# Third down product moved ahead of the fourth up product, TensorE's block loop turned by half a block, and the last block taken out of the loop

## The chip, the core and the metric

The kernel runs on one core of a Trainium2 chip. The metric is device time in microseconds (us) of one execution. Three runs of the kernel before took 1391.1, 1392.65 and 1392.87 us; the median is 1392.65 us.

## The reference

One layer of a streaming encoder over 512 tokens of width 1024, with 16 learned meta tokens in front. After the attention half comes a mixture of 32 experts, and the change lies in this second half:

```python
def clamped_swiglu(hu):
    gate, lin = hu[..., :D_FF], hu[..., D_FF:]
    gate = jnp.minimum(gate, SWIGLU_LIMIT)
    lin = jnp.clip(lin, -SWIGLU_LIMIT, SWIGLU_LIMIT)
    return gate * jax.nn.sigmoid(SWIGLU_ALPHA * gate) * (lin + 1.0)

def moe(h, w_router, b_router, w1, b1, w2, b2):
    ...
    top_val, top_idx = lax.top_k(logits, TOP_K)          # 4 of 32 experts for each token
    gates = jax.nn.softmax(top_val, axis=-1)
    ...
    def expert_block(args):
        tok, e = args
        xb = xf[tok]
        act = clamped_swiglu(xb @ w1[e] + b1[e])
        return act @ w2[e] + b2[e]
```

The weighted results are added to the token rows, and a final RMS norm gives the output. `w1[e]` is 1024 x 2048 and `w2[e]` is 1024 x 1024, both float32: 8 MB and 4 MB for each expert, all of them read once.

## The kernel before, in words

**Blocks.** The tokens of an expert are cut into blocks of 32 rows. With the given inputs there are 81 blocks, numbered 0 to 80 (`nb` is 81; the page of the profile counts 81 of the instruction on L1308, which runs once for each block). Experts stand in an order worked out on the chip; an expert's position in it is its *place*, 0 to 31. Place 0 holds three blocks here (0, 1 and 2), place 1 two (3 and 4), place 2 three (5, 6 and 7), and the last place one (block 80).

**Weights.** Two sets of buffers in SBUF hold the weights of an even place and of an odd place (`par` 0 and 1). A place's weights come in six transfers of 2 MB, issued by the SP queue strictly in order: four quarters of w1 (L508) and then two halves of w2 (L513). Each waits until TensorE has read the same part of the place two before for the last time: quarter c of w1 for `w1_read`, which an up product raises four times; the first half of w2 for `w2_read`, which a down product raises in its middle; and the second half for `y_done`, which it raises at its end. A transfer that waits holds up all behind it in the queue.

**One block's work.** GpSimd gathers 32 token rows (`gather`, L600). VectorE turns them to the layout TensorE needs (`turn_rows`, L1255, into the one buffer `xT`). TensorE forms the up product (`up`, L1816, 64 instructions, and the bias products on L1826) in a PSUM bank. VectorE and ScalarE apply the clamped SwiGLU (`hidden`, L1308 to L1314, and `sigmoid`, L849). VectorE turns the result into the one buffer `actT` (`turn_hidden`, L1301). TensorE forms the down product (`down`, bias on L1846, 64 instructions on L1854). VectorE and ScalarE scale it (`outputs`, `high_outputs`), and GpSimd adds it to the rows in DRAM (`scatter`, L609). The last two blocks are not scattered: their rows stay in SBUF (`quarters_kept`, L1321) and are spread by one-hot products after the loop (L1906).

**Lists.** For each block a small chain makes the list of its tokens: VectorE compares (`slot_list`, L1217 and L1221), TensorE sums (`slot_product`, L1786), VectorE makes the indices (`slot_rows`, L1236 to L1249).

**Order on TensorE.** Written u for up, d for down and s for slot_product, the order is u0 u1 u2 d0 d1 u3, and then a loop over pairs of blocks in which `pe_block(g)` is s(g+3), d(g), u(g+2). `up_of` and `down_of` choose by a branch between code for an even and for an odd place (L1833, L1862), each some 130 instructions long. The loop has a fixed number of rounds, for the largest number of blocks that could be (MAXBLK is 95). Rounds past the last block only test (L1894) and count (L1892).

**Order on VectorE.** `dve_block(g)` is hidden(g+1), which also turns the rows of block g+2, slot_rows(g+3), turn_hidden(g+1), outputs(g), quarters_kept(g), slot_list(g+4), selector(g+2). `selector` fills a small tile that TensorE's bias products read.

**After the loop.** TensorE waits for `hot_ready` (the one-hot tiles of `last_places`) and for `y_kept`, and runs the 64 products on L1906. The sums with the rows that came back from DRAM, the norm and the output follow.

Of the kernel before, what the change touches and what calls it, by code (L numbers as in the profile page):

```python
# [27 lines left out]
ALU = mybir.AluOpType  # L28
AX = mybir.AxisListType

P = 128
D = 1024
# [7 lines left out]
NE, TOPK = 32, 4  # L40
SLOTS = 32
# [92 lines left out]
def build(nc, I, out):  # L134
    ctx = ExitStack()
    with ctx:
# [770 lines left out]
        def _(dve):  # L907
# [343 lines left out]

            def turn_rows(b, r):

                dve.wait_ge(xg_in[b], r * 16 + 16)
                nc.vector.transpose(xT.rearrange("p (c j) s -> p c j s", j=2),  # L1255
                                    xg[b].rearrange("p (c q j) -> p c j q", c=Q, j=2)).then_inc(xT_ready, 1)
# [26 lines left out]
            turn_rows(0, 0)  # L1283
            step(nc.vector.scalar_tensor_tensor(ptab[:, :], prow[:, 2:NG], float(AHEAD), prow[:, 0:NG - 2],
                                                ALU.mult, ALU.add))
# [5 lines left out]
            def selector(n, b):  # L1291

                nc.vector.tensor_scalar(selb[:, b, :], ca[:, C_EXP:C_EXP + 1].to_broadcast([P, SLOTS]),
                                        egf[:, bass.ds(n, 1)], None, ALU.is_equal).then_inc(sel_ready, 1)

            def turn_hidden(n, b):
# [7 lines left out]
            def hidden(n, b, r):  # L1304

                gate, lin = PS[:, b, 0:QD], PS[:, b, QD:2 * QD]
                dve.wait_ge(up_done, n + 1)
                nc.vector.tensor_scalar(gat[b], gate, HID_LIMIT, None, ALU.min).then_inc(gat_ready, 1)  # L1308
                turn_rows(1 - b, r)
                nc.vector.tensor_scalar(lin, lin, HID_LIMIT, -HID_LIMIT, ALU.min, ALU.max).then_inc(hid_step, 1)  # L1310
                dve.wait_ge(sig_ready, n + 1)
                nc.vector.tensor_tensor(gat[b], gat[b], PS[:, 2 + b, 0:QD], ALU.mult).then_inc(hid_step, 1)
                dve.wait_ge(hid_step, 2 * n + 2)
                nc.vector.scalar_tensor_tensor(gat[b], lin, 1.0, gat[b], ALU.add, ALU.mult).then_inc(act_ready, 1)  # L1314

            def quarters_kept(n, b, last=False):

                dve.wait_ge(y_done, n + 1)
                if not last:
                    dve.wait_ge(y_high, 2 * n + 2)  # L1320
                nc.vector.tensor_scalar(gat[b], PS[:, 4 + 2 * b, 0:QD], gates[:, bass.ds(n, 1)], None, ALU.mult)\  # L1321
                    .then_inc(y_kept, 1)

# [40 lines left out]
            def final_norm():  # L1364

                n0 = step.n
                for t in range(TT):
# [18 lines left out]
            slot_list(2)  # L1386
            nc.vector.tensor_scalar(selb[:, 2, :], ca[:, C_EXP:C_EXP + 1].to_broadcast([P, SLOTS]),
                                    egf[:, 2:3], None, ALU.is_equal).then_inc(sel2_ready, 1)
# [17 lines left out]
            def dve_block(g, b, i):  # L1406

                with dve.If(g + 1 < nb):
                    hidden(g + 1, 1 - b, i + 1)
                    slot_rows(g + 3, 1 - b, i + 2 if b else i + 1)  # L1410
                    turn_hidden(g + 1, 1 - b)
                    outputs(g, b)
                    quarters_kept(g, b)
                    slot_list(g + 4)
                    selector(g + 2, b)
                with dve.Else():
                    last_places()
                    quarters_kept(g, b, last=True)
                    final_norm()
                dve.nop()  # L1420

            with dve.Fori(1, (MAXBLK + 1) // 2) as i:
                g = 2 * i
                with dve.If(g < nb):
                    dve_block(g, 0, i)
                    with dve.If(g + 1 < nb):
                        dve_block(g + 1, 1, i)
                    dve.nop()
                dve.nop()
# [3 lines left out]
        def _(pe):  # L1433
# [372 lines left out]
            def group(c):  # L1806
                return slice(c * SLOTS, (c + 1) * SLOTS)

            def up(g, at_place, par, b, s=None, listed=None):

                w = w1t(par).rearrange("p k (a c n) -> p k a c n", a=4, c=Q)
                for k in range(KT):
                    if k % 2 == 0:
                        pe.wait_ge(w1_full[par][k // 2], (at_place // 2) * 16 + 16)
                    for c in range(Q):
                        last = mm(PS[group(c), b, :].rearrange("p (a n) -> p a n", a=4),  # L1816
                                  xT[:, k, :], w[:, k, :, c, :], start=k == 0, stop=False)
                    if k % 2 == 1:
# [10 lines left out]

            def up_of(g, at_place, b, s=None, listed=None):  # L1830

                pe.wait_ge(xT_ready, g + 1)
                with pe.If(at_place % 2 == 0):  # L1833
                    up(g, at_place, 0, b, s, listed)
                with pe.Else():
                    up(g, at_place, 1, b, s, listed)
                pe.nop()

            def down(g, at_place, par, b):

                pe.wait_ge(sel_ready, g + 1)
                if not (isinstance(g, int) and g < 2):
                    pe.wait_ge(y_high, 2 * g - 2)
                y = PS[:, 4 + 2 * b, 0:QD]
                for n in range(Q):
                    mm(y[group(n), :], selb[:, b, :], ball[:, 2 * D + n * QD:2 * D + (n + 1) * QD],  # L1846
                       start=True, stop=False)
# [24 lines left out]
            nb = pe.value_load(btabi[0:1, NE - 1:NE], min_val=TOPK * T // SLOTS, max_val=MAXBLK)  # L1872
            second = places_of(0)[1]
            first, third = places_of(1)
            up_of(1, first, 1, listed=3)
            pe.wait_ge(sel2_ready, 1)
            pe.wait_ge(act_ready, 1)
            up_of(2, second, 0, 2, listed=4)
            down(0, 0, 0, 0)
            down_of(1, first, 1)  # L1880
            up_of(3, third, 1)

            def pe_block(g, b):

                here, following = places_of(g)
                slot_product(g + 3)
                down_of(g, here, b)
                with pe.If(g + 2 < nb):
                    up_of(g + 2, following, b)
                pe.nop()  # L1890

            with pe.Fori(1, (MAXBLK + 1) // 2) as i:  # L1892
                g = 2 * i
                with pe.If(g < nb):  # L1894
                    pe_block(g, 0)
                    with pe.If(g + 1 < nb):
                        pe_block(g + 1, 1)
                    pe.nop()
                pe.nop()

            pe.wait_ge(hot_ready, 2)
            pe.wait_ge(y_kept, nb)
# [36 lines left out]
```

## Time and profile before

| | |
|---|---|
| median of three runs | 1392.65 us |
| the profiled execution | 1391.69 us |
| its span, first to last instruction | 1389.8 us |
| TensorE busy (PE) | 1261.3 us, 91% |
| VectorE busy (DVE) | 688.0 us, 49% |
| read from HBM | 440.13 MB |
| start of up product 0 | 369.37 us |
| start of the products on L1906 | 1370.36 us |

Times inside the profile count from the start of the span. The part from 369 us to 1366 us is the expert part. PE rows are matmuls and PEld rows are weight loads on the same engine. A time in square brackets is the idle time of the engine before the row, with what ended it; "issue" there means that the profile shows nothing that the engine waited for. PEclk is the granted share of TensorE's clock, 1.00 or 0.50 (2.4 or 1.2 GHz) or a mean of the two.

### The profile page before, as it was taken

How to read it: one execution, taken by the hardware profiler on the slowest of the kernel's cores; microseconds unless marked ns; L12 is line 12 of the kernel's file. 1: busy time of each engine (PE TensorE's matmuls, PEld its weight loads, DVE VectorE, ACT ScalarE, POOL GpSimd, SP SyncE). 2: the span in 40 equal slices, each digit the busy share in tenths (PEclk: the TensorE clock that was granted, in tenths of full speed). 3: DMA queues.
4: the chain of work that ended last, by engine and by line, in shares of the span. 5: the costliest groups of instructions: out<-in, count | busy, mean ns of one | idle time of the engine just before them, and what ended most of it. 6: DMA issues, size and time to landing. Idle time of an engine off the chain costs nothing.

```text
span 1389.8 us, 36015 instructions
## 1 busy us (share of the span) xinstructions
PE 1261.3 (91%) x13054; PEld 547.4 (39%) x13055; DVE 688.0 (49%) x2297; ACT 316.7 (23%) x575; POOL 298.4 (21%) x466
## 2 busy tenths in 40 slices
PE   7999999989589995999899989995999799989983
PEld 4656666555233331333233333331333233333332
DVE  2113333663735552565456645652656256645654
ACT  2012223433112220222122212220222022212212
POOL 5310000002212220222122312220222123312221
PEclk9999999999799997999999999997999899999996
DMA  9520002509778999999999999999999999999994
GB/s 327 148 58 1 1 0 86 222 23 383 306 301 359 417 417 425 417 419 418 417 419 417 419 417 375 403 419 422 416 419 418 422 416 421 416 418 419 417 420 168
DMA packets 51671, 458.87 MB, mean 330 GB/s; under 512 B 8629, under 2 KB 9013, under 8 KB 27061
## 3 DMA queue, kind: packets, MB, share of 16 engines
q1 hardware_dynamic: 43316, 436.38, 75.6%
q0 software_dynamic: 7936, 21.71, 5.9%
q8 instruction: 23, 0.38, 0.1%
q10 hardware_dynamic: 384, 0.32, 0.1%
q14 instruction: 12, 0.09, 0.0%
HBM read 440.13 MB, written 18.25 MB: 330 GB/s over the span
## 4 chain that ended last, share of the span: by engine, by line
PE 73%; DMA 20%; DVE 4%; issue 2%; ACT 1%; POOL 0%; DVEq 0%; ACTq 0%; SPq 0%; POOLq 0%
PE PS L1816 33%; DMA sb_arena<-in_w 19%; PE PS L1854 16%; PE PS L1489 4%; PE PS L1483 4%; PE PS L1486 2%; PE PS L1487 2%; PE PS L1683 2%; PE PS L1826 1%; PE PS L1846 1%; PE PS L1534 1%; DMA xfd<-sb_arena 1%; PE PS L1656 1%; PE PS L1786 1%; PE PS L1586 1%
## 5 line engine op out<-in xcount | busy, mean ns | idle before, releaser
L1816 PE MATMUL PS<-sb_arena,sb_work 128*32 128x512 f32 x5184 | 599.1, 612 | 67.8 <-DMA sb_arena<-in_w 61.7
L1816 PEld LDWEIGHTS PS<-sb_arena,sb_work 128*32 128x32 f32 x5184 | 158.1, 112 | 454.5 <-issue 355.7
L1854 PE MATMUL PS<-sb_arena,sb_work 128*32 128x256 f32 x5184 | 297.4, 382 | 3.6 <-issue 2.8
L1308 DVE TENSOR_SCALAR sb_work<-PS 128x256 f32<-128x256 f32 x81 | 34.4, 425 | 356.7 <-PE PS L1826 356.7
L1854 PEld LDWEIGHTS PS<-sb_arena,sb_work 128*32 128x32 f32 x5184 | 156.3, 111 | 114.4 <-issue 7.7
L849 ACT ACTIVATE PS<-sb_work 128x256 f32<-128x256 f32 x81 | 31.4, 388 | 518.8 <-DVE sb_work L1308 518.8
L857 ACT ACTIVATE sb_work<-PS,sb_gates 32x256 f32<-32x256 f32 x160 | 75.0, 469 | 257.8 <-PE PS L1854 252.6
L609 POOL DMA_INDIRECT accd<-sb_work,sb_sidc x79 | 113.6, 1438 | 33.4 <-issue 33.4
L617 POOL TENSOR_TENSOR sb_sm<-sb_sm 128x1 f32<-128x1 f32 x79 | 15.4, 195 | 489.0 <-DMA accd<-sb_work,sb_sidc 489.0
L888 ACT ACT_TABLE_LOAD x79 | 101.4, 1283 | 1.4
L1217 DVE TENSOR_SCALAR sb_slots<-sb_ca,sb_b,sb_rk 128x128 bf16<-128x128 f32 x332 | 92.6, 342 | 3.0 <-issue 3.0
L600 POOL DMA_INDIRECT sb_work<-xfd,sb_gidx x82 | 84.1, 1026 | 38.0 <-issue 36.1
L1301 DVE STREAM_TRANSPOSE sb_work<-sb_work 128x256 f32<-128x256 f32 x81 | 54.0, 667 | 59.2 <-PE PS L1854 59.1
L1330 DVE TENSOR_SCALAR sb_work<-PS,sb_gates 32x256 f32<-32x256 f32 x160 | 74.2, 464 | 3.9
L1483 PE MATMUL PS<-sb_arena 128*128 128x512 f32 x128 | 58.7, 600 | 1.2 <-DVE sb_arena L950 1.2
L1489 PE MATMUL PS<-sb_arena 128*128 128x512 f32 x128 | 58.6, 598 | 1.0 <-DVE sb_arena L972 1.0
L1003 DVE TENSOR_TENSOR_SCAN sb_arena<-sb_arena 128x1344 f32<-128x1344 f32 x8 | 23.7, 2957 | 70.2 <-ACT sb_arena L718 70.2
L1255 DVE STREAM_TRANSPOSE sb_work<-sb_work 128x256 f32<-128x256 f32 x82 | 36.1, 440 | 15.5 <-DMA sb_work<-xfd,sb_gidx 15.2
L599 POOL TENSOR_TENSOR sb_sm<-sb_sm 128x1 f32<-128x1 f32 x82 | 15.9, 194 | 128.8 <-DVE sb_gidx L1247 116.3
L1321 DVE TENSOR_SCALAR sb_work<-PS,sb_gates 128x256 f32<-128x256 f32 x79 | 38.2, 484 | 5.9 <-PE PS L1854 3.3
L1486 PE MATMUL PS<-sb_arena 128*128 128x264 f32 x128 | 39.3, 389 | 0.0
L1786 PEld LDWEIGHTS PS<-sb_g6c,sb_slots 128*128 128x128 bf16 x336 | 14.0, 97 | 63.2 <-issue 54.6
(274 smaller groups left out, 1166.4 us busy)
## 6 DMA issues: line engine op xcount, KB each, us to landing
sb_arena<-in_w SPq DMA_DIRECT2D x192, 2048.0 KB, 24.1
sb_arena<-in_w_in SPq DMA_DIRECT2D x6, 2048.0 KB, 20.7
sb_arena<-in_x SPq DMA_DIRECT2D x8, 512.0 KB, 8.2
sb_arena<-in_w_out SPq DMA_DIRECT2D x2, 2048.0 KB, 11.8
accd<-sb_arena SPq DMA_DIRECT2D x4, 512.0 KB, 9.2
xfd<-sb_arena SPq DMA_DIRECT2D x4, 512.0 KB, 6.5
sb_arena<-accd SPq DMA_DIRECT2D x4, 512.0 KB, 13.0
out<-sb_arena SPq DMA_DIRECT2D x4, 512.0 KB, 2.7
```

What stands on the lines that cost most here:

```text
L600: pool.indirect_dma_start(out=xg[b], out_offset=None, in_=xfd, in_offset=bass.IndirectOffsetOnAxis(ap=gidx[:, b:b + 1], axis=0)).then_inc( ...
L609: pool.indirect_dma_start(out=acc, out_offset=bass.IndirectOffsetOnAxis(ap=sidc[0:SLOTS, b:b + 1], axis=0), in_=yb[b], in_offset=None, com ...
L857: act.activation(yb[b][:, c * QD:(c + 1) * QD], PS[rows, 4 + 2 * b, 0:QD], ACT.Copy, scale=gates[rows, bass.ds(n, 1)]).then_inc(y_high, 1)
L888: act.preload_act_table(ACT.Sigmoid)
L1217: nc.vector.tensor_scalar(slots[:, t, :].rearrange("p (q s) -> p q s", s=SLOTS), ca[:, C_SLOT:C_SLOT + SLOTS].unsqueeze(1).to_broadcast([P ...
L1301: nc.vector.transpose(actT.rearrange("p (c j) s -> p c j s", j=4), gat[b].rearrange("p (c q j) -> p c j q", c=2, j=4)).then_inc(actT_ready, 1)
L1330: nc.vector.tensor_scalar(yb[b][:, c * QD:(c + 1) * QD], PS[rows, 4 + 2 * b, 0:QD], gates[rows, bass.ds(n, 1)], None, ALU.mult).then_inc(y ...
L1483: last = mm(PS[:, b, :], w[:, k, f * P:(f + 1) * P], nT[:, k, META:NKEY], **io)
L1486: mm(PS[:, b, 0:n], w[:, k, f * P:(f + 1) * P], nT[:, k, 0:n], **io)
L1489: last = mm(PS[:, b, :], nT[:, k, META + f * P:META + (f + 1) * P], w[:, k, :], **io)
L1816: last = mm(PS[group(c), b, :].rearrange("p (a n) -> p a n", a=4), xT[:, k, :], w[:, k, :, c, :], start=k == 0, stop=False)
L1854: last = mm(y[group(n), :], actT[:, k, :], w[:, k, n * QD:(n + 1) * QD], start=False, stop=k == KT - 1)
```

## The change

TensorE's order in the opening becomes u0 u1 u2 d0 d1 **d2** u3 s5. The loop then runs over odd g first, and `pe_block(g)` is u(g+1), s(g+3), d(g). From u4 on this is the same sequence as before (u4 s6 d3 u5 s7 d4 ...), up to the end: before it was u80 s82 d79 s83 d80, now it is s82 d79 inside the loop, and u80 d80 written out behind it for an odd place. u80 and d80 use PSUM banks 7 and 0 and a spare selector tile.

On VectorE the rows of block 1 are turned into `actT`, which is free at that time, before hidden(0), and the rows of block 2 into `xT` right after hidden(0). In `dve_block`, slot_list(g+4) moves from behind quarters_kept to ahead of turn_hidden. The last but one block's round becomes hidden(80), turn_hidden(80), quarters_kept(79), last_places, quarters_kept(80), final_norm.

```diff
@@ VectorE, opening
-            hidden(0, 0, 0)
-            turn_hidden(0, 0)
+            turn_rows(1, 0, actT)
+            hidden(0, 0)
+            turn_rows(0, 1)
             slot_rows(3, 1, 1)
             slot_list(4)
-            hidden(1, 1, 1)
+            hidden(1, 1)
+            turn_hidden(0, 0)
             slot_rows(4, 0, 2)
@@ VectorE, one block
-                with dve.If(g + 1 < nb):
+                with dve.If(g + 2 < nb):
                     hidden(g + 1, 1 - b, i + 1)
                     slot_rows(g + 3, 1 - b, i + 2 if b else i + 1)
+                    slot_list(g + 4)
                     turn_hidden(g + 1, 1 - b)
                     outputs(g, b)
                     quarters_kept(g, b)
-                    slot_list(g + 4)
                     selector(g + 2, b)
                 with dve.Else():
+                    spare_selector(g + 1)
+                    hidden(g + 1, 1 - b, bank=7)
+                    turn_hidden(g + 1, 1 - b)
+                    quarters_kept(g, b)
                     last_places()
-                    quarters_kept(g, b, last=True)
+                    quarters_kept(g + 1, 1 - b, last=True)
                     final_norm()
@@ TensorE, opening
-            up_of(1, first, 1, listed=3)
+            up_of(1, first, 1, listed=3, rows=actT)
             pe.wait_ge(sel2_ready, 1)
             pe.wait_ge(act_ready, 1)
             up_of(2, second, 0, 2, listed=4)
             down(0, 0, 0, 0)
             down_of(1, first, 1)
+            down_of(2, second, 0)
             up_of(3, third, 1)
+            slot_product(5)
@@ TensorE, one block and the loop
                 here, following = places_of(g)
+                with pe.If(g + 2 < nb):
+                    up_of(g + 1, following, 1 - b)
+                pe.nop()
                 slot_product(g + 3)
                 down_of(g, here, b)
-                with pe.If(g + 2 < nb):
-                    up_of(g + 2, following, b)
-                pe.nop()
...
-            with pe.Fori(1, (MAXBLK + 1) // 2) as i:
-                g = 2 * i
-                with pe.If(g < nb):
-                    pe_block(g, 0)
-                    with pe.If(g + 1 < nb):
-                        pe_block(g + 1, 1)
+            with pe.Fori(1, MAXBLK // 2) as i:
+                g = 2 * i + 1
+                with pe.If(g + 1 < nb):
+                    pe_block(g, 1)
+                    with pe.If(g + 2 < nb):
+                        pe_block(g + 1, 0)
...
+            pe.wait_ge(xT_ready, nb)
+            pe.wait_ge(sel2_ready, 2)
+            up(nb - 1, NE - 1, 1, 7, s=2)
+            down(nb - 1, NE - 1, 1, 0, s=2, bank=0)
             pe.wait_ge(hot_ready, 2)
             pe.wait_ge(y_kept, nb)
```

The table of places (`ptab`) now holds the place of block g+1 beside that of block g, where it held that of g+2.

## Rows read from the trace of the kernel before

**Rows 1.** The page: the DMA engines in 40 slices, and a group of instructions.
```profile
DMA  9520002509778999999999999999999999999994
...
L1816 PE MATMUL PS<-sb_arena,sb_work 128*32 128x512 f32 x5184 | 599.1, 612 | 67.8 <-DMA sb_arena<-in_w 61.7
```

**Rows 2.** Timeline of TensorE, the opening: start us, us, engine, line [idle].
```profile
381.00 3.64 PE L1816 MATMUL PS<-sb_arena,sb_work 128*32 128x512 f32 x32 [1.49 <-DVE sb_work L1255]
...
390.02 3.64 PE L1816 MATMUL PS<-sb_arena,sb_work 128*32 128x512 f32 x32 [1.40 <-DVE sb_work L1255]
...
402.06 3.66 PE L1854 MATMUL PS<-sb_arena,sb_work 128*32 128x256 f32 x64 [0.76 <-DVE sb_work L1301]
408.78 8.68 PE L1816 MATMUL PS<-sb_arena,sb_work 128*32 128x512 f32 x64 [3.06 <-issue]
...
421.40 7.58 PE L1816 MATMUL PS<-sb_arena,sb_work 128*32 128x512 f32 x63
```

**Rows 3.** Timeline of GpSimd, and its DMA issues from 371 to 376 us, to landing.
```profile
372.87 1.00 POOL L600 DMA_INDIRECT sb_work<-xfd,sb_gidx  x1 [0.47 <-issue]
```
```profile
sb_work<-xfd,sb_gidx POOLq DMA_INDIRECT x1, 7.0
```

**Rows 4.** Timeline of VectorE, the opening: block 2's rows are turned.
```profile
389.00 0.43 DVE L1255 STREAM_TRANSPOSE sb_work<-sb_work 128x256 f32<-128x256 f32 x1
```

**Rows 5.** Source view of L1833, whole span: nanoseconds min/median/max, first and last start.
```profile
L1833 PEldq COMPARE_BRANCH  x121: 66/177/3881, 380.6 to 1339.5; - x121
```

**Rows 6.** Timeline of the SP queue: transfers for places 2 and 4.
```profile
420.02 2.06 SPq L513 DMA_DIRECT2D sb_arena<-in_w  x2
...
460.72 5.49 SPq L508 DMA_DIRECT2D sb_arena<-in_w  x4
```

**Rows 7.** Issue to landing, the transfers issued at 420.02, 460.72 and 847.31 us.
```profile
sb_arena<-in_w SPq DMA_DIRECT2D x1, 2048.0 KB, 9.5
```
```profile
sb_arena<-in_w SPq DMA_DIRECT2D x1, 2048.0 KB, 11.0
```
```profile
sb_arena<-in_w SPq DMA_DIRECT2D x1, 2048.0 KB, 8.5
```

**Rows 8.** One microsecond: engines' busy us, PEclk, DMA share, GB/s.
```profile
416.00:417.00 1.00, 1.00 (x16) 0.35 (x12) 0.00 (x0) 0.00 (x0) 0.00 (x0) 1.00 0.09 16
```

**Rows 9.** Timeline of TensorE, the end.
```profile
1340.10 5.35 PE L1816 MATMUL PS<-sb_arena,sb_work 128*32 128x512 f32 x48
1349.37 1.92 PE L1816 MATMUL PS<-sb_arena,sb_work 128*32 128x512 f32 x16 [3.92 <-DMA sb_arena<-in_w]
...
1359.76 5.92 PE L1854 MATMUL PS<-sb_arena,sb_work 128*32 128x256 f32 x64
1370.36 5.82 PE L1906 MATMUL PS<-sb_work,sb_arena 32*128 32x256 f32 x64 [4.68 <-issue]
```

**Rows 10.** Timeline of VectorE, the end.
```profile
1320.60 1.11 DVE L1217 TENSOR_SCALAR sb_slots<-sb_ca,sb_b,sb_rk 128x128 bf16<-128x128 f32 x4
...
1339.38 0.15 DVE L1249 TENSOR_TENSOR sb_sidx<-sb_c 128x1 f32 x1
...
1351.56 0.42 DVE L1308 TENSOR_SCALAR sb_work<-PS 128x256 f32<-128x256 f32 x1 [7.62 <-PE PS L1826]
...
1353.00 0.42 DVE L1314 SCALAR_TENSOR_TENSOR sb_work<-PS,sb_work 128x256 f32<-128x256 f32 x1
...
1361.32 0.43 DVE L1341 CAST sb_arena<-sb_sidx 128x1 f32 x2 [2.28 <-DMA sb_arena<-in_final_norm]
...
1365.88 0.48 DVE L1321 TENSOR_SCALAR sb_work<-PS,sb_gates 128x256 f32<-128x256 f32 x1 [3.34 <-PE PS L1854]
```

**Rows 11.** Source view of L1892 from 1365 to 1371 us: the loop's count.
```profile
L1892 PEldq FUSED_REGOPS  x7: 35/35/41, 1365.2 to 1369.7; - x7
```

**Rows 12.** Two stretches at the end, with PEclk third from the right.
```profile
1350.00:1355.00 5.00, 5.00 (x90) 2.34 (x80) 2.95 (x12) 0.39 (x1) 0.20 (x1) 1.00 1.00 429
...
1370.00:1374.00 4.00, 3.64 (x36) 3.31 (x40) 0.00 (x0) 0.00 (x0) 0.00 (x0) 0.50 0.00 0
```

More of the change, by code:

```diff
@@ L1302, in turn_hidden, with hidden @@
                                     gat[b].rearrange("p (c q j) -> p c j q", c=2, j=4)).then_inc(actT_ready, 1)
[L1304 to L1306 removed]
+            def hidden(n, b, r=None, bank=None):
+                bank = b if bank is None else bank
+                gate, lin = PS[:, bank, 0:QD], PS[:, bank, QD:2 * QD]
                 dve.wait_ge(up_done, n + 1)
                 nc.vector.tensor_scalar(gat[b], gate, HID_LIMIT, None, ALU.min).then_inc(gat_ready, 1)
[L1309 removed]
+                if r is not None:
+                    turn_rows(1 - b, r)
                 nc.vector.tensor_scalar(lin, lin, HID_LIMIT, -HID_LIMIT, ALU.min, ALU.max).then_inc(hid_step, 1)
@@ L1423, in _ @@
                 g = 2 * i
-                with dve.If(g < nb):
+                with dve.If(g + 1 < nb):
                     dve_block(g, 0, i)
-                    with dve.If(g + 1 < nb):
+                    with dve.If(g + 2 < nb):
                         dve_block(g + 1, 1, i)
@@ L1816, in up @@
                         last = mm(PS[group(c), b, :].rearrange("p (a n) -> p a n", a=4),
-                                  xT[:, k, :], w[:, k, :, c, :], start=k == 0, stop=False)
+                                  rows[:, k, :], w[:, k, :, c, :], start=k == 0, stop=False)
                     if k % 2 == 1:
@@ L1828, in up, with up_of, down @@
                 last.then_inc(up_done, 1)
-            def up_of(g, at_place, b, s=None, listed=None):
+            def up_of(g, at_place, b, s=None, listed=None, rows=xT):
                 pe.wait_ge(xT_ready, g + 1)
                 with pe.If(at_place % 2 == 0):
-                    up(g, at_place, 0, b, s, listed)
+                    up(g, at_place, 0, b, s, listed, rows)
                 with pe.Else():
-                    up(g, at_place, 1, b, s, listed)
+                    up(g, at_place, 1, b, s, listed, rows)
                 pe.nop()
[L1839 to L1844, printed above, removed]
+            def down(g, at_place, par, b, s=None, bank=None):
+                if s is None:
+                    pe.wait_ge(sel_ready, g + 1)
+                    if not (isinstance(g, int) and g < 2):
+                        pe.wait_ge(y_high, 2 * g - 2)
+                y = PS[:, 4 + 2 * b if bank is None else bank, 0:QD]
                 for n in range(Q):
-                    mm(y[group(n), :], selb[:, b, :], ball[:, 2 * D + n * QD:2 * D + (n + 1) * QD],
+                    mm(y[group(n), :], selb[:, b if s is None else s, :], ball[:, 2 * D + n * QD:2 * D + (n + 1) * QD],
                        start=True, stop=False)
@@ L1872, in _ @@
             nb = pe.value_load(btabi[0:1, NE - 1:NE], min_val=TOPK * T // SLOTS, max_val=MAXBLK)
-            second = places_of(0)[1]
-            first, third = places_of(1)
-            up_of(1, first, 1, listed=3)
+            first, second = places_of(1)
+            third = places_of(3)[0]
+            up_of(1, first, 1, listed=3, rows=actT)
             pe.wait_ge(sel2_ready, 1)
```

18 lines of the change are left out of this document (10 added, 8 removed).

## The prediction

> **What bounds the kernel now.** I read the page first. Its DMA line in 40 slices [rows 1] shows the DMA engines at nine tenths or more from slice 13 (from about 450 us) to the last but one, and the largest group of matmuls has 61.7 of its 67.8 us of idle time ended by weight transfers. So the expert part is one stream of weights, and TensorE follows it. Time can be won in three places only: ahead of the stretch in which DMA never rests, in a rest that is left, or behind the last weights.
>
> Next I read single microseconds of the DMA share around 416 us. There the engines rest [rows 8], until the halves of w2 for place 2 are issued at 420.02 us [rows 6]; they wait for down product 2, which stands behind up product 3. This is the rest that moving d2 ahead of u3 attacks. Then the timelines of TensorE, VectorE, GpSimd and the SP queue for the opening [rows 2 to 6], and last the end [rows 9 to 12]. There the last quarter of w1 lets u80 finish at about 1351.5 us, d80 runs 5.92 us from 1359.76, and from the last down product (1359.76 + 5.92 = 1365.68) to the products on L1906 (1370.36) lie 4.68 us marked "issue" [rows 9]. The source view of L1892 says what they are: TensorE's sequencer counts through the seven empty rounds of its loop, from 1365.2 to 1369.7 [rows 11], 0.75 us a round.
>
> **The opening, step by step.** The two waits ahead of u1 and u2 are 1.49 and 1.40 us [rows 2].
> - u1: its rows now go to a free buffer, so u0 need not have ended. But the gather of block 1 lands 7.0 us after 372.87, at 379.87 [rows 3]. Turning takes 0.43 us [rows 4] and TensorE starts 0.59 us after that (389.43 to 390.02 [rows 2, 4]): 380.9 for 381.00. Saves 0.1, taken as nothing.
> - u2: block 2's rows are turned while u1 runs. The whole 1.40 us go: u2 starts at 388.6.
> - d0 and d1: 1.40 earlier; d1 at 400.66 to 404.3.
> - d2 now follows d1 at once, and `actT` is one buffer: the turning that d1 waited 0.76 us for is exposed again. d2 runs from 405.1 to 408.75. It releases w2 of place 2 at about 407, 13 us earlier than 420.02.
> - u3: in before it started 6.72 us after d1 (402.06 to 408.78 [rows 2]), because the branch to its code for an odd place took 3.88 us, the longest of the 121 on that line [rows 5]; it fills the gap ahead of u3. The same jump now follows d2: 405.1 + 6.72 = 411.8, and with 8.68 us and 0.2 for the bias, its end is 420.7.
> - u4 now follows u3 directly. Its rows can only be turned once u3 has read `xT`, which d2 used to cover. That is the 1.40 us of u2 again [rows 2]: u4 at 422.1, against 421.40 in before.
>
> So TensorE comes out of the opening 0.7 us *later*, although DMA got two transfers 13 us ahead. From u4 on the order is that of before. The following transfers wait for TensorE's reads (w1 of place 3 for u4, w2 of place 3 for d4, w1 of place 4 for u7), so the rest of DMA moves rather than goes. The tightest is the issue at 460.72. It landed 11.0 us later, while an issue into an idle queue landed after 9.5 (at 420.02) and 8.5 (at 847.31) [rows 6, 7]. So that transfer had 1.5 to 2.5 us of queue ahead of it, and no more than this can be taken out. With the issue 0.7 us later, 0.8 to 1.8 us are left; I take 1.3. From there DMA is the bound, TensorE takes over its shift at the long wait near 540 us, and 1.3 us go through to the end. Bounds: the 3.88 us branch cost TensorE 3.06 us of idle time and some 1.6 of half clock behind it (u3 took 8.68; an up product without that takes 5.35 + 1.92 less 0.2 of overlap, 7.1 [rows 2, 9]). If it doesn't recur, the opening gives 1.3 + 4.7 = 6.0; if a second one comes, 1.3 - 4.7 = -3.4.
>
> **The loop.** Sequence and number of rounds as before: nothing. Moving slot_list ahead of turn_hidden delays `actT` and the scatter by some 1.8 us a block (1.11 of compares [rows 10], and an estimated 0.7 for the copy and the register steps). I cost it at nothing: an up product of 7 us runs meanwhile, and `actT` is due at its end. Without that cover it would be 1.8 us a block.
>
> **The end, on the clock of before.** d78 ends at 1340.10. d79 no longer waits behind u80.
> - VectorE has block 81's indices at 1339.53 [rows 10], then slot_list 1.8, then the turning, some 0.7: `actT` at 1342.1. d79 runs 3.65 us, to 1345.8.
> - The seven empty rounds: TensorE's next product starts 4.7 us after the last one's end, as in before [rows 9, 11]: u80 at 1350.5. The last quarter of w1 landed at 1349.3 [rows 9], so it no longer waits for DMA.
> - u80 takes 7.3 us at full clock, bias included, to 1357.8. Ahead of it TensorE is idle for 4.7 us. After 3.06 us of idle time u3 lost 1.6 us, after 3.92 us the clock stayed 1.00, and d80 in before lost 2.3 (5.92 for the 3.66 of d1) [rows 2, 9, 12]. Between 0 and 2.3 I take 1.6. So 1359.4.
> - hidden(80) takes 1.86 us (1351.56 to 1353.42 [rows 10]) and is now exposed, with the turning and TensorE's start 0.8: 1362.1. The second half of w2 was there for d80 at 1359.76 in before [rows 9], so d80 waits for no weights.
> - d80 3.6 us: 1365.7, as in before. The last rows are kept 0.7 us later, 1366.4. The one-hot tiles, which wait for the final gain at 1361.3 [rows 10], are ready by 1364.
> - L1906 starts at 1366.5 where it started at 1370.36: **3.9 us**, all from the empty rounds that now lie elsewhere. It ran at half clock in before [rows 12]; if it runs at full clock, its first half is up to 1.9 us shorter. I take 1.0. Sum of the end 4.9; bounds 0.9 (2.3 of half clock for u80 and again for d80, L1906 no faster) and 7.4 (none).
>
> **Sum.** 1.3 + 4.9 = 6.2 us. The profiled execution took 1391.69 us, 0.96 below the median. 1391.69 - 6.2 = 1385.5, against the median 1386.4.
>
> **The rivals.**
> 1. *The rest of DMA stays filled.* For it: the cold branch may fall elsewhere. Against it: u4 then still waits for its rows. 6.0 + 4.9: 1381.8.
> 2. *The opening loses.* A second cold branch among d2, u3, u4. -3.4 + 4.9: 1391.2.
> 3. *The end gains nothing.* u80 and d80 are new code that runs once. A stall of 3.88 us [rows 5] there, in the place of the empty rounds saved, leaves 1.0, and with half clock after it -1.3: with the opening's 1.3, 1390.3 to 1392.6. Against it: u0 and d0 were straight code too, and ran without such a gap.
> 4. *Slower.* Instruction fetch stalls at each new piece of code: once more in the opening (-3.4) and twice at the end (2 x 3.88, and 2.3 of half clock each, -12.4 + 4.9 = -7.5): 1403.6. It decides from the second stall at the end on; with one it is rival 3. Against it: the median branch on that line took 0.18 us [rows 5].
>
> The Trainium skill ("Runtime: NRT & Kernel Launch", Instruction fetch mechanics) says that prefetch is purely sequential and that a taken branch out of the window held forces a fetch. By that rule rival 4 would be the rule, not the exception. The trace agrees for one branch of 3.88 us only; the empty rounds, which jump over the whole loop body, take 0.75 us each with four instructions.
>
> **How the numbers follow.** Forecast 0.58 (own range 1383 to 1389.5), rival 1 0.12, rival 2 0.07, rival 3 0.16, rival 4 0.07. A measurement of this kernel can tell some 0.2%, 2.8 us: faster is below 1389.9, slower above 1395.4. Faster: 0.58 + 0.12 and a quarter of rival 3, 0.04: 0.74. Same 0.19, slower 0.07. Range 1381.5 to 1391.3: it holds the forecast, rivals 1 and 2 by their middle, and the near part of rival 3.
>
> **What would show it.** In the profile after: the w2 issue now near 420 stands near 407; u1 still at 381, u2 at 388.6; a branch near 4 us ahead of u3; 1.4 us idle with VectorE's turning ahead of u4, and u4 near 422; a short rest of DMA between 445 and 465 us. The long waits for weights (near 540, 675, 800) keep their sizes within 1 us or so. At the end u80 starts some 4.7 us behind d79 and does not wait for DMA, u80 to d80 shows 2.7 us, and less than 1 us lies between d80 and L1906. Wrong would be: a u4 earlier than 420, a stall inside u80 or d80, or a `sel_ready`, `y_high` or `added` that comes late through the moved slot_list.

## The result, and the profile after

The changed kernel takes 1402.68 us (median of 11 runs, 1398.07 to 1408.42), the kernel before 1392.87 us (11 runs, 1389.62 to 1397.98). The ratio is 1.007, with a 95% interval of 1.0052 to 1.0089: slower by some 10 us, where 6 us faster was predicted. The profiled execution took 1403.72 us, its span 1401.9.

The stages, in us, cut at the same products in both timelines of TensorE (u80, d80 and L1925 of the kernel after are the last rows shown below):

| stage | before | after | difference |
|---|---|---|---|
| start of the span to u0 | 369.37 | 367.22 | -2.15 |
| u0 to u4 | 52.04 | 52.81 | +0.77 |
| u4 to the end of d6 | 48.33 | 56.68 | +8.35 |
| end of d6 to the end of d78 | 870.54 | 880.74 | +10.20 |
| end of d78 to the end of the span | 49.56 | 44.43 | -5.13 |

The first line is the attention half, which the change doesn't touch; it varied from 365.0 to 372.0 in the profiles of this study. So the opening up to u4 and the end did what was predicted of them (+0.7 and -4.9), and some 18.5 us (8.35 and 10.20) were lost between them, where the prediction had seen no loss.

What took them stands in the view of waits, TensorE, from 440 to 1350 us (waiting line, releaser: us in total, times, longest). Before:

```profile
PE PS L1816 <- DMA sb_arena<-in_w: 61.7, 20, 10.3
PE PS L1846 <- issue: 0.2, 1, 0.2
```

And after, where L1828 is the up product (L1816 before) and L1859 the bias of the down product (L1846 before):

```profile
PE PS L1828 <- issue: 36.0, 57, 1.0
PE PS L1828 <- DMA sb_arena<-in_w: 28.3, 12, 4.6
PE PS L1859 <- issue: 3.6, 1, 3.6
```

The waits for weights fell by half, and yet the kernel is slower: TensorE now starts 57 up products late, and nothing that it waited for is shown. The page after shows the DMA engines in 40 slices, the shares of the chain that ended last (before: PE 73%, DMA 20%, issue 2%), and the group of the up product. The first and the last line of before are [rows 1].

```profile
DMA  9520002518897899999999997999999999999994
...
PE 80%; DMA 9%; issue 5%; DVE 4%; ACT 1%; POOL 0%; DVEq 0%; ACTq 0%; POOLq 0%; SPq 0%
...
L1828 PE MATMUL PS<-sb_arena,sb_work 128*32 128x512 f32 x5184 | 590.4, 606 | 74.2 <-issue 41.6
```

The releaser of the largest group has changed from DMA (61.7) to issue (41.6), and the DMA line has a 7 in its 25th slice, where before it was all nines from the 14th to the last but one.

**Where a late start comes from.** The timeline of TensorE, after, three blocks near the end of the loop (a turn of the loop holds two):

```profile
1319.25 3.63 PE L1867 MATMUL PS<-sb_arena,sb_work 128*32 128x256 f32 x64
1323.32 7.07 PE L1828 MATMUL PS<-sb_arena,sb_work 128*32 128x512 f32 x64 [0.44 <-issue]
...
1330.85 3.63 PE L1867 MATMUL PS<-sb_arena,sb_work 128*32 128x256 f32 x64
1335.10 7.07 PE L1828 MATMUL PS<-sb_arena,sb_work 128*32 128x512 f32 x64 [0.62 <-issue]
...
1346.30 7.07 PE L1828 MATMUL PS<-sb_arena,sb_work 128*32 128x512 f32 x64
```

The same in the kernel before:

```profile
1292.86 3.63 PE L1854 MATMUL PS<-sb_arena,sb_work 128*32 128x256 f32 x64
1296.32 7.04 PE L1816 MATMUL PS<-sb_arena,sb_work 128*32 128x512 f32 x64
1303.18 0.39 PE L1826 MATMUL PS<-sb_ball,sb_selb 128*32 128x512 bf16 x4
...
1307.26 5.32 PE L1816 MATMUL PS<-sb_arena,sb_work 128*32 128x512 f32 x48
```

Before, an up product starts 0.17 us before the modelled end of the down product (1292.86 + 3.63 = 1296.49), and a block takes 10.94 us (1296.32 to 1307.26). After, two blocks take 11.78 and 11.20 us (1323.32 to 1335.10 to 1346.30). The source views of the sequencer's own steps (nanoseconds min/median/max, first and last start) say why. The loop's test, then the load of the places, then the branch into the up product, after, from 1332 to 1336 us:

```profile
L1907 PEldq COMPARE_BRANCH  x1: 211/211/211, 1333.1 to 1333.1; - x1
...
L1814 PEldq TENSOR_LOAD <-sb_ptab x1: 305/305/305, 1333.8 to 1333.8; - x1
...
L1845 PEldq COMPARE_BRANCH  x1: 80/80/80, 1334.8 to 1334.8; - x1
```

And the load of the kernel before, from 1299 to 1304 us:

```profile
L1802 PEldq TENSOR_LOAD <-sb_ptab x1: 486/486/486, 1301.2 to 1301.2; - x1
```

TensorE's sequencer, the part that hands instructions to the engine, runs ahead of its matmuls. It is past the last one of this down product some 1.5 us before the product ends (L1907 begins at 1333.0, the product ends at 1334.48). The steps from there to the next product take 2.1 us (1333.0 to 1335.10), and 0.62 is exposed. Before, the load at 1301.2 lies under an up product that runs to 1303.36 and its bias products on L1826, which run to 1303.57. The sequencer's first step behind them (L1896) begins at 1300.8, so it is some 2.8 us ahead, and nothing is exposed. The turn moved the loop's count and tests and the load of places from behind an up product to behind a down product. No product and no round was added.

**From u4 to d6.** The timeline of TensorE after, opening:

```profile
402.79 0.63 PE L1867 MATMUL PS<-sb_arena,sb_work 128*32 128x256 f32 x6 [0.75 <-DVE sb_work L1306]
404.94 5.30 PE L1867 MATMUL PS<-sb_arena,sb_work 128*32 128x256 f32 x58 [1.52 <-issue]
411.10 7.09 PE L1828 MATMUL PS<-sb_arena,sb_work 128*32 128x512 f32 x64 [0.86 <-issue]
...
420.02 7.07 PE L1828 MATMUL PS<-sb_arena,sb_work 128*32 128x512 f32 x64 [1.43 <-DVE sb_work L1255]
...
432.31 4.26 PE L1867 MATMUL PS<-sb_arena,sb_work 128*32 128x256 f32 x43 [3.30 <-issue]
...
447.62 0.40 PE L1859 MATMUL PS<-sb_ball,sb_selb 128*32 128x256 bf16 x4 [3.56 <-issue]
447.80 6.24 PE L1867 MATMUL PS<-sb_arena,sb_work 128*32 128x256 f32 x64
```

Before, a stall lies inside d3 as well:

```profile
433.72 2.96 PE L1854 MATMUL PS<-sb_arena,sb_work 128*32 128x256 f32 x49 [2.82 <-issue]
```

The branch source views of `up_of` and `down_of`, whole span (`up_of` before is [rows 5]):

```profile
L1845 PEldq COMPARE_BRANCH  x120: 80/177/2427, 378.5 to 1350.8; - x120
```
```profile
L1875 PEldq COMPARE_BRANCH  x120: 63/169/5888, 396.0 to 1361.5; - x120
```

The branch ahead of u3 is there (2.43 us), and there is a second one: 5.89 us ahead of d4, where `down_of` had at most 0.42 us before. TensorE stands for 3.56 us and then runs d4 at half clock for nearly all of its length, 6.24 us in place of 3.63.

The profile also counts DMA packets of the kind `instruction`, some 16 KB each; for which engine they are it doesn't say. The DMA view of the kernel after has one from 429 to 434 us, in the stall inside d3, and from 455 to 1367 us, the loop once its code has run a few times, no line of that kind:

```profile
q8 instruction: 1, 0.02, 1.3%
```
```profile
q1 hardware_dynamic: 24345, 354.58, 91.3%
q0 software_dynamic: 7134, 19.53, 8.2%
```

Such packets start at 402.49, 408.58, 429.92 and 445.10 us. The matmuls behind the four stalls, in d2, ahead of u3, in d3 and ahead of d4, start 2.4 to 2.5 us after them each time. Others, at 414.90, 421.38 and 436.35, lie under running products and cost nothing. So these stalls coincide with loads of code, at a branch or, as in d3, in straight code. The late starts in the loop do not: no such packet comes there.

The SP queue after:

```profile
408.37 2.37 SPq L513 DMA_DIRECT2D sb_arena<-in_w  x2
422.15 5.47 SPq L508 DMA_DIRECT2D sb_arena<-in_w  x4
451.63 2.94 SPq L513 DMA_DIRECT2D sb_arena<-in_w  x2
467.68 2.08 SPq L508 DMA_DIRECT2D sb_arena<-in_w  x2
```

The first w2 issue came ahead, from 50.65 to 41.15 us after u0 [rows 6], but the second came later, and the issue that was at 460.72 stands at 467.68: 9.1 us later against u0. From 412 to 420 us the share of the DMA engines rose from 0.47 to 1.01, as meant. From 444 to 456 us it is (second from the right), before and then after:

```profile
444.00:456.00 12.00, 12.00 (x164) 4.79 (x168) 6.79 (x24) 3.00 (x5) 3.08 (x5) 1.00 1.01 418
```
```profile
444.00:456.00 12.00, 8.31 (x91) 3.51 (x92) 5.84 (x22) 2.13 (x4) 1.43 (x3) 0.72 0.46 149
```

The rest that was filled near 416 us is back near 450.

**The end**, timeline of TensorE after (before is [rows 9]):

```profile
1358.62 0.26 PE L1798 MATMUL PS<-sb_g6c,sb_slots 128*128 128x6 bf16 x4 [1.17 <-DVE sb_g6c L1221]
...
1359.29 3.66 PE L1867 MATMUL PS<-sb_arena,sb_work 128*32 128x256 f32 x64
1367.62 8.77 PE L1828 MATMUL PS<-sb_arena,sb_work 128*32 128x512 f32 x64 [4.68 <-issue]
...
1379.20 3.66 PE L1867 MATMUL PS<-sb_arena,sb_work 128*32 128x256 f32 x64 [2.48 <-DVE sb_work L1306]
1383.66 3.74 PE L1925 MATMUL PS<-sb_work,sb_arena 32*128 32x256 f32 x64 [0.80 <-DVE sb_work L1328]
```

### The profile page after: what moved, and what is told of

Its sections match the earlier page's. It is cut to its first block, busy times and chain, and to the rows that moved or that the text cites. A ratio compares the mean times of both kernels' runs of the same rounds, so it can differ in the third digit from the quotient of the medians.

```text
span 1401.9 us, 35786 instructions
## 1 busy us (share of the span) xinstructions
PE 1264.4 (90%) x13050; PEld 558.5 (40%) x13051; DVE 674.9 (48%) x2281; ACT 316.6 (23%) x575; POOL 294.2 (21%) x466
## 4 chain that ended last, share of the span: by engine, by line
PE 80%; DMA 9%; issue 5%; DVE 4%; ACT 1%; POOL 0%; DVEq 0%; ACTq 0%; POOLq 0%; SPq 0%
PE PS L1828 38%; PE PS L1867 19%; DMA sb_arena<-in_w 7%; PE PS L1501 4%; PE PS L1495 4%; PE PS L1498 2%; PE PS L1499 2%; PE PS L1695 2%; PE PS L1838 1%; PE PS L1859 1%; PE PS L1798 1%; PE PS L1546 1%; PE PS L1668 1%; PE PS L1598 1%; DMA xfd<-sb_arena 1%
## 5 line engine op out<-in xcount | busy, mean ns | idle before, releaser
L1828 PE MATMUL PS<-sb_arena,sb_work 128*32 128x512 f32 x5184 | 590.4, 606 | 74.2 <-issue 41.6
L1828 PEld LDWEIGHTS PS<-sb_arena,sb_work 128*32 128x32 f32 x5184 | 168.7, 111 | 457.1 <-issue 411.3
L1867 PE MATMUL PS<-sb_arena,sb_work 128*32 128x256 f32 x5184 | 301.1, 385 | 8.8 <-issue 4.8
L1867 PEld LDWEIGHTS PS<-sb_arena,sb_work 128*32 128x32 f32 x5184 | 158.5, 111 | 121.7 <-issue 13.5
L857 ACT ACTIVATE sb_work<-PS,sb_gates 32x256 f32<-32x256 f32 x160 | 74.9, 468 | 260.9 <-PE PS L1867 233.6
L609 POOL DMA_INDIRECT accd<-sb_work,sb_sidc x79 | 107.5, 1360 | 35.2 <-issue 35.2
L1498 PE MATMUL PS<-sb_arena 128*128 128x264 f32 x128 | 39.3, 389 | 0.0
L1499 PE MATMUL PS<-sb_arena 128*128 128x264 f32 x128 | 39.0, 386 | 0.0
```

The source lines that it names most:

```text
L609: pool.indirect_dma_start(out=acc, out_offset=bass.IndirectOffsetOnAxis(ap=sidc[0:SLOTS, b:b + 1], axis=0), in_=yb[b], in_offset=None, com ...
L857: act.activation(yb[b][:, c * QD:(c + 1) * QD], PS[rows, 4 + 2 * b, 0:QD], ACT.Copy, scale=gates[rows, bass.ds(n, 1)]).then_inc(y_high, 1)
L1498: mm(PS[:, b, 0:n], w[:, k, f * P:(f + 1) * P], nT[:, k, 0:n], **io)
L1499: last = mm(PS[:, b + 1, 0:n], w[:, k, f * P:(f + 1) * P], nT[:, k, n:NKEY], **io)
L1867: last = mm(y[group(n), :], actT[:, k, :], w[:, k, n * QD:(n + 1) * QD], start=False, stop=k == KT - 1)
```

## The experiments

The theory after this profile was that the turn of the loop cost most. Rivals were the new order of products (d2 ahead of u3), the moved slot_list, and the end. The third experiment was run once; each of the others has an interval against the kernel before, measured beside it. The first four ran on one chip, where the kernel before took 1393.49 us, and the last five on another, where it took 1393.38 us and, beside e9, 1392.56. A difference of two experiments' medians below is good to some 3 us. "Late starts" are idle times ahead of a product that are marked "issue".

**e1_wrap_behind_up.** The kernel after, with its order of products, but u4 ahead of the loop, so that the loop's count and the load stand behind an up product again.

```diff
+            up_of(4, fourth, 0)
@@ one block
                 here, following = places_of(g)
-                with pe.If(g + 2 < nb):
-                    up_of(g + 1, following, 1 - b)
-                pe.nop()
                 slot_product(g + 3)
                 down_of(g, here, b)
+                with pe.If(g + 3 < nb):
+                    up_of(g + 2, following, b)
+                pe.nop()
```

> The changed kernel with every product in the same order, but u4 ahead of the loop and the loop's body s(g+3), d(g), u(g+2): the loop's count, its tests and the load of the places stand behind the long up product again. Theory (the sequencer's steps are exposed behind the short down product): the idle time marked issue ahead of the up products, 36.8 us between 465 and 1335 us in the changed kernel, falls under 3 us, and the kernel takes 1385 to 1390 us, below the kernel before. Rival 1 (the moved slot_list makes the loop slow): 1400 us or more, gaps with VectorE as releaser. Rival 2 (cold code in the opening and at the end costs it): 1397 us or more, since all that code is still there.

Measured: 1390.79 us, ratio 0.9984 (0.9965 to 1.0003), 0.8 us outside what was expected. From the end of d6 to the end of d78 the late starts of up products fell from 35.8 to 1.9 us, as expected. The turn was worth 11.9 us (1402.68 less 1390.79); the order of products isn't the main loss.

**e2_slot_list_back.** The kernel after, slot_list(g+4) back behind quarters_kept.

```diff
-                    slot_list(g + 4)
                     turn_hidden(g + 1, 1 - b)
                     outputs(g, b)
                     quarters_kept(g, b)
+                    slot_list(g + 4)
```

> The changed kernel with slot_list(g+4) back behind quarters_kept. Theory (sequencer's steps exposed): no change, 1401 to 1405 us, the same gaps of 0.2 to 1.0 us ahead of the up products. Rival 1 (slot_list): 1388 to 1394 us.

Measured: 1405.46 us, ratio 1.0093 (1.0062 to 1.0125), 0.5 us above the range. The moved list isn't the loss. Its stage from d78 to the end took 48.12 us, against 44.43: the move is part of the gain at the end.

**e3_place_load_twice.** The kernel after, with the load of places done twice in each block: a larger dose of the suspected cost.

```diff
+                places_of(g)
                 here, following = places_of(g)
```

> The changed kernel with the place load of a block made twice. Theory: one load with its register steps is 0.77 us of the sequencer's time (1345.08 to 1345.86 in the changed kernel), it lies on the path ahead of 77 up products, and takes the place of the waits for weights that are left (28.3 us) first: 35 to 60 us more, 1435 to 1463 us, with gaps of 0.8 to 1.8 us. If the sequencer's steps were hidden, or weights the bound: no more than 5 us more.

Measured: 1433.26 us in a single run, 30.6 above the kernel after, 1.7 below the range. The waits of TensorE from 440 to 1380 us:

```profile
PE PS L1828 <- issue: 86.0, 72, 1.7
PE PS L1828 <- DMA sb_arena<-in_w: 19.5, 9, 3.3
```

77 further loads (156 in place of 79) added 50.0 us of late starts, 0.65 us each, and made 72 up products late in place of 57. From d6 to d78 the stage grew by 32.3 us: 48.0 more of late starts, less 8.8 of waits for weights, less 6.2 of busy time (17.1 us of that stage ran at half clock, 30.7 in the kernel after), and less 0.6 of gaps under 0.15 us. The range had reckoned with 0.77 us a load.

**e4_end_alone.** The kernel before, with only the last block's products behind the loop (`spare_selector`, bank 7 and 0, `up(nb - 1, ...)`, `down(nb - 1, ...)` and the last but one round of VectorE, as in the change). The excerpt shows TensorE's part.

```diff
                 down_of(g, here, b)
-                with pe.If(g + 2 < nb):
+                with pe.If(g + 3 < nb):
                     up_of(g + 2, following, b)
...
+            up(nb - 1, NE - 1, 1, 7, s=2)
+            down(nb - 1, NE - 1, 1, 0, s=2, bank=0)
```

> The kernel before with the last block's two products behind the loop and nothing else (opening, loop phase and slot_list as before). Theory: the end gives what the two profiles show from the last-but-two down product to the end, 5.3 us (49.7 for 44.4 us): 1386.5 to 1389 us. Rival (the gain of the end is only seen because the weights came earlier than TensorE there, and is lost when u80 waits for them): 1391 to 1394 us.

Measured: 1389.77 us, ratio 0.9981 (0.9961 to 1.0002), 0.8 us above the range. The stage from d78 on took 49.18 us, against 49.56 before: almost nothing was won. Its timeline of TensorE:

```profile
1340.18 0.26 PE L1797 MATMUL PS<-sb_g6c,sb_slots 128*128 128x6 bf16 x4 [3.66 <-DVE sb_g6c L1221]
...
1340.75 5.35 PE L1866 MATMUL PS<-sb_arena,sb_work 128*32 128x256 f32 x64
```

With slot_list in its place of before, the list for s82 is late, TensorE idles 3.66 us, and d79 runs in part at half clock (5.35 us in place of 3.66).

**e5_one_load_hidden.** The kernel after, with the second block's load of places behind the first block's up product; the one at the loop's turn stays behind the down product.

```diff
+                up_of(g + 1, following, 0)
+                after = places_of(g + 1)[1]
+                slot_product(g + 3)
+                down_of(g, here, 1)
...
+                    with pe.If(g + 3 < nb):
+                        up_of(g + 2, after, 1)
```

> The changed kernel, still turned, but the place load for the second block of a pair stands right behind the first block's up product (its result is kept in a register), so behind one of two down products only a branch and a wait are left. Theory (what counts is the time of the sequencer's steps behind a down product against its lead of some 1.5 us): the gaps of 0.2 to 0.45 us ahead of every second up product vanish, those of 0.6 to 1.0 us at the loop's wrap stay, 11 to 14 us of gaps go, and with the waits for weights that grow in their place the kernel takes 1392 to 1397 us. Rival (the gaps come from instruction fetch at the wrap and the branches): 1400 us or more, both kinds of gap still there.

Measured: 1396.36 us, ratio 1.0019 (1.0002 to 1.0036). 6.3 us are back, about half of the turn's cost. Timeline of TensorE:

```profile
1302.37 7.07 PE L1828 MATMUL PS<-sb_arena,sb_work 128*32 128x512 f32 x64 [0.99 <-issue]
...
1313.35 7.04 PE L1828 MATMUL PS<-sb_arena,sb_work 128*32 128x512 f32 x64
...
1325.12 7.07 PE L1828 MATMUL PS<-sb_arena,sb_work 128*32 128x512 f32 x64 [0.66 <-issue]
...
1336.10 7.04 PE L1828 MATMUL PS<-sb_arena,sb_work 128*32 128x512 f32 x64
```

Every second block takes 10.98 us again, as before, and the one across the loop's turn 11.77. From d6 to d78 the late starts fell by 7.7 us (from 35.8 to 28.1, 56 to 34 of them), where 11 to 14 were expected; the stage is 8.5 us shorter (872.21 us). The end gives 3.1 us of it back (47.48 us against 44.43). From the start of d79 to u80 lie 10.67 us in place of 8.33.

**e6_end_and_list.** e4 with slot_list(g+4) ahead of turn_hidden.

```diff
+                    slot_list(g + 4)
                     turn_hidden(g + 1, 1 - b)
                     outputs(g, b)
                     quarters_kept(g, b)
-                    slot_list(g + 4)
```

> The kernel before with its own opening and loop order, the last block's products behind the loop, and slot_list ahead of turn_hidden. Theory (the move of slot_list serves the end: without it the last but one down product waits 3.66 us for the list and starts the low clock): from the end of d78 to the end 44.4 us for 49.2 of the end alone, 1385.5 to 1388.5 us. Rival (slot_list's place does not matter): 1389 to 1391 us.

Measured: 1386.04 us, ratio 0.9947 (0.993 to 0.9964). The end's gain comes with the list's move: d78 to the end 45.28 us, against 49.18 in e4.

**e7_opening_no_branch.** e1, with u1 to u4, d1 and d2 written out for the places that these inputs give (right for these inputs alone), so that the opening has neither branches nor code for the other kind of place.

```diff
-            up_of(1, first, 1, listed=3, rows=actT)
+            pe.wait_ge(xT_ready, 2)
+            up(1, 0, 0, 1, listed=3, rows=actT)
...
-            down_of(1, first, 1)
-            down_of(2, second, 0)
-            up_of(3, third, 1)
+            down(1, 0, 0, 1)
+            down(2, 0, 0, 0)
+            pe.wait_ge(xT_ready, 4)
+            up(3, 1, 1, 1)
```

> The kernel with the wrap behind the up product, and its opening (u1, u2, d1, d2, u3, u4) written for the places that these inputs give, without branches and without the code of the other parity. Theory (the 4 us branch ahead of u3 is instruction fetch at a jump): u3 follows d2 within 0.2 us at full clock, 4 to 5 us less from u0 to u4 than the 53.7 us with branches; 2 to 6 us of it reach the end: 1385 to 1389 us. Rival (the gap ahead of u3 is a wait for something else, or the fetch stall only moves to the first branch of the loop): u0 to d6 no shorter, 1390 to 1392 us.

Measured: 1382.18 us, ratio 0.9899 (0.9877 to 0.9921), 2.8 us better than expected. From u0 to u4 it takes 46.55 us, e1 53.70: the branches of the opening and the code that they jump over cost 7 us up to u4, and 8.6 us in the full runs (1390.79 less 1382.18). u3 follows d2 without a gap, at full clock (7.05 us), and nothing idles inside d2. A branch of 2.33 us remains at 437.11 us.

**e8_rows_in_actT.** e6, with block 1's rows turned into `actT`; d2 still behind u3. The excerpt is against the kernel before.

```diff
-            hidden(0, 0, 0)
-            turn_hidden(0, 0)
+            turn_rows(1, 0, actT)
+            hidden(0, 0)
+            turn_rows(0, 1)
...
-            up_of(1, first, 1, listed=3)
+            up_of(1, first, 1, listed=3, rows=actT)
```

> As the kernel before with the new end and the moved slot_list, and block 1's rows turned into the free buffer, d2 still behind u3. Theory: u2 no longer waits, 1.40 us less from u0 to u4 (50.6 for 52.0), none given back ahead of u4, and as the weights' queue is at its limit up to u7 all of it goes through: 1.4 us below the kernel without it, 1384.5 to 1387 us. Rival: the opening's time is set by the weights, no difference to the kernel without it.

Measured: 1385.69 us, ratio 0.9936 (0.9916 to 0.9955), not to be told from e6. From u0 to u4 it takes 50.97 us, e6 51.86: 0.9 less, where 1.4 was expected. e6 and e8 are the fastest versions here that hold for any inputs; e8 has all of the change except d2's place and the turn of the loop.

**e9_turn_alone.** The kernel after, with d2 behind u3 as before. Its products are those of e8 in the same order.

```diff
-            down_of(2, second, 0)
             up_of(3, third, 1)
             slot_product(5)
+            down_of(2, second, 0)
```

> The kernel after with d2 and s5 in their places of before (u3, s5, d2, then the turned loop from u4 on). TensorE's sequence of products is that of the eighth experiment (e8_rows_in_actT, 1385.69 us); only what the loop's count, its tests and the place load stand behind differs: the short down product here, the up product there. Theory (the turn is the main loss, by itself, whatever the opening does): 1393 to 1400, with some 40 us of 'issue' gaps ahead of the up products and d6 to d78 8 to 12 us longer than in e8. The opening's part (d2 ahead of u3) is then what is left to the kernel after, 3 to 8 us. Rival (the late starts only cost because d2 ahead of u3 has moved the weight stream; with the opening of before they hide in the waits for weights): 1384 to 1389.

Measured: 1398.82 us, ratio 1.0041 (1.0025 to 1.0057). The turn by itself costs 13.1 us (against e8), 11.65 of it from d6 to d78 in the profiles. Its waits of TensorE, 440 to 1350 us, and then those of e8:

```profile
PE PS L1828 <- issue: 36.4, 58, 1.0
PE PS L1828 <- DMA sb_arena<-in_w: 27.9, 12, 4.6
```
```profile
PE PS L1829 <- DMA sb_arena<-in_w: 40.8, 17, 6.5
PE PS L1799 <- issue: 8.5, 15, 0.9
...
PE PS L1860 <- issue: 4.8, 21, 0.3
```

e9 has the late starts of the kernel after with the opening of before: the rival falls. What is left to the kernel after is d2's place, 3.9 us (1402.68 less 1398.82); in the other loop it is 5.1 (e1 less e8). The first is barely clear of the noise: the two intervals, 1.0052 to 1.0089 and 1.0025 to 1.0057, overlap. By ratios to the kernel before the turn costs 12 to 15 us and d2's place 4 to 7.

## Why the prediction was wrong

**The step that failed: "The loop. Sequence and number of rounds as before: nothing."** It counted products and rounds, and not what stands between two products on TensorE's own sequencer. Of what the turn moves, the steps of L1907 and L1814 were to be priced. The trace of before had the means: a load of places beside each block, and a first view of the sequencer was even read, for the empty rounds [rows 11], where 0.75 us a round is the price of the loop's tests with no product to hide them. The turn itself costs 13.1 us (e9 against e8), 11.9 with the other opening (after against e1); hiding one of its two loads takes 6.3 back (e5), and doubling the loads adds 30.6 (e3, one run).

**Why it was not absorbed.** The prediction held that "from there DMA is the bound", so that late starts of TensorE would vanish in its waits for weights. From the end of d6 to the end of d78, idle time before products that is marked "issue" rose from 0.2 to 35.8 us and waits for weights fell from 57.8 to 28.3. The busy time rose by 3.4, by far less than 56 late starts at 0.17 us of lost overlap come to, as 30.7 us of the stage ran at half clock in place of 64.9. Gaps under 0.15 us rose by 0.6: 35.6 - 29.5 + 3.4 + 0.6 = 10.2 after rounding, the stage's loss. So most was absorbed, but 61.7 us of waits were no cover for 36 us of late starts. The waits were 20 stops inside only eight up products: u13 14.3 us, u48 15.3, u58 11.3, and u12, u24, u35, u69 and u80 0.9 to 6.2 each. After, those of the last five are gone and three are left, at u13 9.1, u48 10.9 and u58 8.3. That is also against the prediction's sign that the long waits near 540, 675 and 800 us keep their sizes. The late starts stood at 57 products. Where a place has several blocks, TensorE sets the pace, and a transfer two places on is issued by its reads. I read this last link from the kernel's waits and the fallen DMA rate (416 GB/s from 465 to 1340 us before, 411 from 465 to 1347 after); no run took it apart.

**The opening.** u4 was predicted 52.7 us after u0 and came at 52.81. In this profile the path was another: d2 stopped for 1.52 us after six instructions and went on largely at half clock (5.30 us for 58), the branch ahead of u3 took 2.43 us, and u3 ran at full clock, 7.09 us in place of 8.68. That is not fixed: e2, e3 and e5 have the same opening and branches of 4.33, 3.26 and 4.20 us there, besides a stop of 1.3 to 1.7 us inside d2, and e2 took 54.68 us from u0 to u4. So the branch of near 4 us was foreseen rightly and the stop inside d2 was not, and that the sum came out within 0.1 us is in part luck. The w2 issue came 9.5 us earlier against u0, not 13, since d2 itself was late.

**"TensorE takes over its shift", and 1.3 us go through.** This term was wrong in sign. It took u4 on as before, and bounded a second cold branch at a loss of 3.4 us in total, "among d2, u3, u4". The long branch came at d4, behind the stretch that was looked at. Of the 8.35 us that the stage from u4 to d6 lost, 1.2 lie ahead of u5, 3.7 between u5 and d4 (the stall of 3.56) and 2.9 in d4 (half clock). It delays the issue of w2 for place 3, and DMA rests again.

But this branch is not by itself the price of d2's place. e9, with d2 as before, has one of 5.5 us near 438 us too, idles 3.58 us and runs d4 in 6.31; only nothing stops inside its d3, and d4 starts 74.4 us after u0 (74.9 before, 80.6 after). e2, with the opening of the kernel after, does not stop in d3 either, but 3.14 us ahead of u3, with half clock behind it. e1 (d2 ahead, loop as before) has a branch of 4.3 us near 444 us; e4, e6, e8 and the kernel before have none at d4. The sum over the opening is steadier than its parts. From u0 to the end of d6 the turned loop takes 107.1 to 109.5 us with d2 ahead (after, e2, e3, e5) and 103.5 without (e9); the other loop 105.2 (e1) and 99.8 to 102.4 (before, e4, e6, e8). So rival 2 was right that the opening loses, and in the full runs d2's place costs 3.9 to 5.1 us. What decides which load of code stops TensorE stays open.

**The moved slot_list**, costed at nothing, was right for the loop, as e2 is no faster. But it was no neutral edit: without it the end gains 0.4 us of its 5 (e4, 49.18 us). The prediction put the list in the end's chain (1.8 us ahead of `actT`) and never asked when it would come in its old place. In e6 and e8 the loop also shows small late starts ahead of the list and down products, 13.3 us in e8 (8.5 and 4.8) and 13.1 in e6. e4 has none, and e6 differs from it only in the list's place, so they come with the move. They cost no measurable time (d6 to d78 870.02 us in e6, 869.24 in e4); how they arise wasn't looked at.

**The end** was right in size and in its steps. Predicted and measured: d78 to d79 2.0 and 1.83; the empty rounds ahead of u80 4.7 and 4.68; u80 to d80 11.6 and 11.58; d80 to the last product less than 1 and 0.80; the products now on L1925 at full clock, 3.74 us where they took 5.82 [rows 9]. Sum 4.9 predicted, 5.13 measured.

**The rivals.** Rival 4 gave 1403.6, near the result, but by fetch stalls at the end that did not come; of its three stalls one was real, the long branch in the opening. At the end an instruction packet comes at 1374.6 us, while u80 runs, and nothing stalls. The Trainium skill ("Runtime: NRT & Kernel Launch", Instruction fetch mechanics) has prefetch purely sequential, with a fetch for every taken branch out of the window. The trace agrees only in part: of the 240 branches on L1845 and L1875 the median took 0.17 to 0.18 us, and the ones of 1.7 to 5.9 us all begin ahead of 442 us, while code is reached for the first times. From 450 to 1370 us the 226 branches on these lines take at most 0.23 us, and no instruction packet comes. e7, without the opening's branches and the code that they jump over, shows that the two are worth 7 us up to u4.

## What to carry to other kernels

Before turning or rotating a loop, list what the sequencer of the bound engine does at the turn (count, tests, register loads, branches), and put it behind the longest run of queued work: what costs nothing behind an up product of 7 us cost 0.2 to 1.0 us a time behind a down product of 3.6 us. Waits that sit in eight products out of 81 don't cover a cost that recurs at nearly every block, even where their sum is larger: compare them place by place. And price a moved step for the place it leaves as well as the one it gets: the list's move, costed at nothing, was what made the end's gain possible.

## What the runs showed of the hardware

- TensorE's sequencer was only some 1.5 us ahead of the end of a 128x256 down product when it reached the loop's steps, and some 2.8 us ahead behind the up product (first step at 1300.8, bias products to 1303.57).
- A load of one value with its register steps took 0.65 us of the sequencer (e3), where the load itself shows 0.30 to 0.49 us.
- Stalls marked "issue" in the opening ended 2.4 to 2.5 us after the start of a 16 KB instruction packet (four in the kernel after); code that had run a few times was not loaded again in 910 us of the loop (no such packet from 455 to 1367 us).
- Gaps of up to 1.7 us ahead of up products did not lower the clock (7.07 us each in e3, where no weights were waited for). After 2.48 us ahead of d80 it stayed full too (3.66 us), and after 3.56 us ahead of d4 and 3.66 us ahead of d79 in e4 those products ran in part at 1.2 GHz (6.24 and 5.35 us). The length of the gap alone doesn't tell: behind the stop of 1.52 us inside d2 the other 58 instructions took 5.30 us in the kernel after, and 3.61 us behind 1.54 us in e2.
